# Depthwise convolution on TensorE in strips of 16 channels and two phases, with phases put back in order by on-chip transfers

## The reference, cut to what matters

```python
for i in range(4):                       # DEPTH, D_MODEL 1024, SEQ 2048, D_FF 2816
    if i % 2 == 0:                       # layers 0 and 2
        h = einsum('bsd,de->bse', x, w_in) + b_in
        val, gate = split(h, 2)
        h = val * sigmoid(gate)
        h = causal_depthwise_conv(h, w_dw)  # width 31
        h = silu(layer_norm(h + b_dw, ln_g, ln_b))
        mix = einsum('bsd,de->bse', h, w_out) + b_out
    else:                                # layers 1 and 3
        mix = (trailing means over 2, 4, 8, 16 positions - x) @ w_grp, scaled
    x = layer_norm(alpha * x + mix)
    x = layer_norm(alpha * x + swiglu(x))
```

## Time and profile before

| what | us |
|---|---|
| median of 3 runs | 2491.88 |
| lowest, highest | 2471.06, 2785.29 |
| the profiled execution | 2470.84 |
| its span (slowest core, 2) | 2469.3 |
| spans of the 8 cores | 2450.0 to 2469.3 |
| PE busy in the span | 2393.7 |
| DVE, ACT, POOL busy | 1532.0, 1115.2, 216.5 |

### The profile page before, as it was taken

How to read it: one execution, slowest core, us unless ns; L and a number is a source line. 1 busy time by engine, 2 the same in 40 slices (tenths; PEclk the granted TensorE clock), 3 DMA queues, 4 the chain that set the end, 5 groups by cost and what they waited for, 6 DMA issues and landing times.

```text
span 2469.3 us, 32261 instructions; the slowest of 8 cores (2450.0 to 2469.3 us)
## 1 busy us (share of the span) xinstructions
PE 2393.7 (97%) x12412; PEld 1076.5 (44%) x12412; DVE 1532.0 (62%) x2372; ACT 1115.2 (45%) x1656; POOL 216.5 (9%) x410
## 2 busy tenths in 40 slices
PE   6988999999999999999999999999999999999996
PEld 2333344444444444444444444444444444444444
DVE  3457577468846883735774726764885588555255
ACT  3556445435353535364463554552636263624033
POOL 1000110000000010000100000001000001010110
PEclk9998999999999999999999999999999999999998
DMA  8895986444544454467744477654444435466653
GB/s 182 203 167 99 166 142 103 75 78 66 92 69 81 69 83 68 81 115 143 125 87 67 77 138 125 124 94 73 70 73 78 79 66 89 71 106 139 98 95 99
DMA packets 112456, 250.35 MB, mean 101 GB/s; under 512 B 12080, under 2 KB 55088, under 8 KB 112304
## 3 DMA queue, kind: packets, MB, share of 16 engines
q0 software_dynamic: 58464, 191.92, 47.0%
q1 hardware_dynamic: 53840, 56.38, 9.9%
HBM read 419.17 MB, written 16.78 MB: 177 GB/s over the span
## 4 chain that ended last, share of the span: by engine, by line
PE 89%; issue 6%; DMA 3%; DVE 1%; POOL 1%; SPq 0%; ACT 0%; DVEq 0%; POOLq 0%; ACTq 0%
PE ps L875 89%; DMA sb_R<-x 1%; DMA sb_x<-ud 1%; DMA sb_wM<-win 0%; DMA sb_wF<-wgu 0%; DMA ud<-sb_ust 0%; POOL sb_wM L346 0%; DVE sb_R L452 0%; DVE sb_R L454 0%; POOL sb_wF L346 0%; SPq L652 0%; ACT sb_xT L783 0%; POOL sb_R L774 0%; SPq L774 0%; DVE sb_lnQ L426 0%
## 5 line engine op out<-in xcount | busy, mean ns | idle before, releaser
L875 PE MATMUL ps<-sb_xT,sb_wF 128*128 128x512 bf16 x5632 | 1235.0, 380 | 4.5 <-ACT sb_xT L467 3.7
L875 PEld LDWEIGHTS ps<-sb_xT,sb_wF 128*128 128x128 bf16 x5632 | 550.0, 98 | 684.0 <-issue 24.8
L875 PE MATMUL ps<-sb_hT,sb_wF 128*128 128x512 bf16 x2640 | 582.6, 379 | 0.0
L553 DVE TENSOR_TENSOR sb_hT<-ps,sb_sgF 128x512 bf16<-128x512 f32 x352 | 243.0, 690 | 452.5 <-PE ps L875 441.9
L551 ACT ACTIVATE sb_sgF<-ps 128x512 f32<-128x512 f32 x352 | 210.0, 597 | 534.1 <-PE ps L875 527.5
L875 PEld LDWEIGHTS ps<-sb_hT,sb_wF 128*128 128x128 bf16 x2640 | 256.6, 98 | 317.8 <-issue 12.5
L417 ACT ACTIVATE sb_lnX<-sb_R 128x512 f32<-128x512 f32 (+1 forms) x231 | 140.6, 614 | 369.1 <-DVE sb_R L532 204.2
L532 DVE TENSOR_TENSOR sb_R<-sb_R,ps 128x512 f32<-128x512 f32 (+1 forms) x264 | 177.0, 670 | 165.5 <-PE ps L875 164.1
L875 PE MATMUL ps<-sb_xT,sb_wM 128*128 128x512 bf16 x1024 | 232.3, 385 | 25.4 <-ACT sb_xT L783 24.3
L346 POOL DMA_DIRECT2D sb_wF<-wgu x198 | 104.7, 529 | 1123.2 <-PE ps L875 1123.2
L478 ACT ACTIVATE sb_R<-sb_R,sb_cst 128x512 f32<-128x512 f32 (+1 forms) x256 | 192.6, 797 | 7.4 <-DVE sb_R L454 6.9
(11 more groups left out here) (85 smaller groups left out, 1299.2 us busy)
## 6 DMA issues: line engine op xcount, KB each, us to landing
sb_wF<-wgu POOLq DMA_DIRECT2D x198, 512.0 KB, 5.1
sb_wF<-wd POOLq DMA_DIRECT2D x120, 352.0 KB, 4.4
sb_x<-ud SPq DMA_DIRECT2D x192, 135.0 KB, 5.9
sb_wM<-win POOLq DMA_DIRECT2D x32, 512.0 KB, 7.4
sb_wM<-wout POOLq DMA_DIRECT2D x32, 512.0 KB, 6.4
ud<-sb_ust SPq DMA_DIRECT2D x64, 128.0 KB, 5.7
y<-sb_R SPq DMA_DIRECT2D x12, 512.0 KB, 8.7
sb_R<-x SPq DMA_DIRECT2D x8, 512.0 KB, 16.6
```

Of the source, the lines that this page charges most:

```text
L553: S.op("dve", lambda e: e.tensor_tensor(out=hT[:, jj, h * NT:(h + 1) * NT], in0=ps[:, bu, :], in1=sgF[:, i, :], op=ALU.mult), reads=[("PS" ...
L875: r = self.e.matmul(*a, **k)
```

## The change

A tap tile is now made of two phases, even and odd positions. The 128 rows of contraction are 2 input phases times 4 shifts times 16 channels; the 32 output columns are 16 channels times 2 output phases. So a strip has 16 channels, there are 8 strips (four side by side, two halves h), and a strip needs 4 steps of 256 columns: 32 matmuls a tile as before, with half the columns.

- DVE writes ust by phase and puts 15 positions of history ahead of each row (three kinds: zeros, from the tile before, from uh). The store writes both phases; ud has a row of its own for each quarter.
- x4 is filled by two loads, one per input phase. Each has the source pattern [1, 4], [8 XW, 16], [1, 8 XW - 4]: four shifts by one element of 16 channels.
- Results stand by (channel, phase) on partitions. ACT evicts each half apart; the norm (`phase_finish`) adds the two halves on DVE, and its matmuls have 256 columns. Silu is two operations per block, and two on-chip transfers per block, issued by SP, put the phases side by side along the row. `conv_out` reads that copy, and DVE adds it to R with a strided view of PSUM.
- Tap weights come in their own tensor `lag` in bf16, by two loads on POOL. The last 16 columns of pooling history move into x4's third buffer.
- A write waits for the readers of a buffer alone where there are any, no more for the last writer too.

```diff
-XW = NT + 28
+XW = NH + 16
...
-            if w in self.last_w:
+            if self.readers.get(w):
+                deps.extend(self.readers[w])
+            elif w in self.last_w:
                 deps.append(self.last_w[w])
-            deps.extend(self.readers.get(w, ()))
...
+            s_, q_, sk, qk = sums(st)
+            for t, k in ((s_, sk), (q_, qk)):
+                S.op("dve", lambda e, t=t: e.tensor_tensor(out=t[:, 0:NH], in0=t[:, 0:NH], in1=t[:, NH:NT],
+                                                           op=ALU.add), reads=k, writes=k, dur=tt(NH))
...
+                e.matmul(ps[:, bm, 0:NH], samem, s_, start=True, stop=True)
+                return e.matmul(ps[:, bq, 0:NH], samem, q_, start=True, stop=True)
...
+                j = (i + 2) % 3
+                S.op("dve", lambda e: e.tensor_copy(out=head, in_=ust[:, j, :, NH:NH + 15]),
+                     reads=[("US", j)], writes=[("UX", i)], dur=0.1)
+            S.op("dve", lambda e: e.scalar_tensor_tensor(
+                out=ust[:, i, :, 15:15 + NH].rearrange("p f n -> p n f"),
+                in0=tgt[:].rearrange("p (n f) -> p n f", f=2), scalar=1.0,
+                in1=vbt[:].rearrange("p (n f) -> p n f", f=2), op0=ALU.add, op1=ALU.mult),
+                reads=[("TG",), ("VB",)], writes=[("US", i)], dur=DV)
...
-            for s in range(4):
-                o = q * NT - 28 - s
-                z = max(0, -o)
-                src = ud[L][c, :, o + z:o + XW].rearrange("(g p) w -> p g w", g=4)
-                S.op("sp", lambda e, s=s, z=z, src=src: e.dma_start(out=x4[s * 32:(s + 1) * 32, i, :, z:XW],
-                                                                    in_=src),
...
+            for f in range(2):
+                row = ud[L][f, c, q]
+                src = bass.AP(row.tensor, row.offset, [[1, 4], [8 * XW, 16], [1, 8 * XW - 4]])
+                S.op("sp", lambda e, f=f, src=src: e.dma_start(out=x4[f * 64:(f + 1) * 64, i, 0:8 * XW - 4], in_=src),
+                     reads=[("UD", L, c, q)], writes=[("X4", i, f)], dma=f"d_x4_{i}_{f}", dur=0.55, size=277000, lat=3.0)
...
+                for h in range(2):
+                    for m in range(4):
+                        for g in range(4):
+                            ins = e.matmul(ps[g * 32:(g + 1) * 32, b, h * NH:(h + 1) * NH], wt[:, m * 8 + 2 * g + h, :],
+                                           x4[:, i, (2 * g + h) * XW + 12 - 4 * m:(2 * g + h) * XW + 12 - 4 * m + NH],
+                                           start=(m == 0), stop=(m == 3))
...
+                for f in range(2):
+                    src = bass.AP(yb.tensor, yb.offset + f * step, [[2 * step, 64], [NH, 2], [1, NH]])
+                    S.op("sp", lambda e, f=f, src=src: e.dma_start(
+                        out=yb[:, NT + f * NH:NT + (f + 1) * NH], in_=src),
+                        reads=[tk], writes=[dk], dma=f"{yt[3]}{c}_{f}", dur=0.55, size=65536)
...
+                rv = rq(c, q).rearrange("p (n f) -> p n f", f=2)
+                S.op("dve", lambda e, b=b, rv=rv: e.tensor_tensor(
+                    out=rv, in0=rv, in1=ps[:, b, :].rearrange("p (f n) -> p n f", f=2), op=ALU.add),
```

More of the change, by code:

```diff
@@ L201, in _columns @@
     add("b2", 8 * DEPTH)
-    add("sel", 32)
+    add("sel", 16)
     add("ones", 128)
+    add("same", 128)
     add("invc", 16)
@@ L206, in _columns @@
         add(f"bin{l}", 16)
[L207 to L210, removed]
+        add(f"bdw{l}", 16)
+        add(f"lng{l}", 16)
+        add(f"lnb{l}", 16)
         add(f"bout{l}", 8)
@@ L621, in conv_in @@
             i = flip("ust", 3)
[L622 to L626, removed]
+            head = ust[:, i, :, 0:15]
+            if q == 0:
+                S.op("dve", lambda e: e.memset(head, 0.0), writes=[("UX", i)], dur=0.1)
+            elif q == 2:
+                S.op("dve", lambda e: e.tensor_copy(out=head, in_=uh[:, c, :, 0:15]),
+                     reads=[("UH", c)], writes=[("UX", i)], dur=0.1)
+            else:
+                j = (i + 2) % 3
[6 more added lines that the diff above has]
+                reads=[("TG",), ("VB",)], writes=[("US", i)], dur=DV)
+            S.op("sp", lambda e: e.dma_start(
+                out=ud[L][:, c, q].rearrange("f k (g w) -> (k g) f w", g=8), in_=ust[:, i]),
+                reads=[("US", i), ("UX", i)], writes=[("UD", L, c, q)], dma=f"d_us{i}", dur=0.45, size=139264, lat=1.0)
+            if q == 1:
+                S.op("dve", lambda e: e.tensor_copy(out=uh[:, c, :, 0:15], in_=ust[:, i, :, NH:NH + 15]),
+                     reads=[("US", i)], writes=[("UH", c)], dur=0.1)
         def conv_taps(q, L, c, bk, yt):
@@ L668, in conv_taps @@
+                return ins
+            S.op("pe", mm, reads=[("X4", i, s) for s in range(2)] + wk, writes=[("PS", b)], dur=1.1)
+            for h in range(2):
+                S.op("act", lambda e, h=h: e.activation(out=y[:, h * NH:(h + 1) * NH], in_=ps[:, b, h * NH:(h + 1) * NH],
+                                                        func=AF.Identity, bias=col(f"bdw{l}", 2 * c + h), scale=1.0),
+                     reads=[("PS", b), ("C0",)], writes=yk[h:h + 1], dur=0.48)
             ln_acc(bk["st"], c, y, yk, (yt[0][0], yt[2][0]))
@@ L673, in out @@
             def out(c):
-                S.op("act", lambda e: e.activation(out=yt[1][c], in_=yt[0][c], func=AF.Silu,
-                                                   bias=col(f"lnb{l}", c), scale=col(f"lng{l}", c)),
-                     reads=yt[2][c] + [("C0",)], writes=yt[2][c], dur=0.86, table="silu")
-            ln_finish(bk["st"], [(yt[0][c], yt[2][c]) for c in range(8)], bk["ln"], out)
+                y, yb, (tk, dk) = yt[0][c], yt[1][c], yt[2][c]
+                for h in range(2):
+                    S.op("act", lambda e, h=h: e.activation(
+                        out=yb[:, h * NH:(h + 1) * NH], in_=y[:, h * NH:(h + 1) * NH], func=AF.Silu,
+                        bias=col(f"lnb{l}", 2 * c + h), scale=col(f"lng{l}", 2 * c + h)),
+                        reads=[tk, ("C0",)] if h == 0 else [tk, dk, ("C0",)], writes=[tk], dur=0.5, table="silu")
+                step = yb.ap[0][0]
+                for f in range(2):
[3 more added lines that the diff above has]
+                        reads=[tk], writes=[dk], dma=f"{yt[3]}{c}_{f}", dur=0.55, size=65536)
+            phase_finish(bk["st"], [(yt[0][c], yt[2][c]) for c in range(8)], bk["ln"], out)
         def conv_out(q, L, bk, yt):
@@ L712, in pool_head @@
                 rk = [*RK(2 * g, q), *RK(2 * g + 1, q)]
-                pk = [("X4", i, s) for s in range(4)]
+                pk = [("X4", i, s) for s in range(2)]
                 if q == 0:
@@ L847, in build @@
         consts()
+        S.op("dve", lambda e: e.memset(ust[:, :, :, XW - 1:XW], 0.0), writes=[("UX", i) for i in range(3)], dur=0.1,
+             boost=9 * BOOST)
         ringM.load()
@@ L950, in _prep @@
     m["cst"] = cst
+    m["lag"] = lags
     for L in layers:
```

119 lines of the change are left out of this document (77 added, 42 removed).

## The result

The changed kernel is slower: a ratio of 1.0421 (95% interval 1.0363 to 1.0479), with a median of 2592.24 us against 2483.96 us for the kernel before. Its profiled execution took 2576.41 us, 1.5 us more than its span, as before. The forecast was 2507 us, "within 2%" its likeliest single outcome. The time lies in the range for 8 in 10 (2415 to 2620), but outside the 2468 to 2560 that the forecast gave for itself, and close to rival 1's 2598. In some executions the cores of one die ran slower, at a lower granted clock than the others: the ratios leave such executions out and the medians do not, and since one die was like that in the profiled execution of three experiments (the product alone, and four engines in one layer only), their rows are of cores of the other die, which are named.

A forecast was written before the change was run, and what follows sets the result against it. PE was taken to bound the dense part, with tap loads on four DMA engines deciding. 2470.84 + 3.6 (dense: 42.3 stalls less 38.7 saved) + 32 (first 300 us) = 2506, say 2507 us; own range 2468 to 2560, 8 in 10: 2415 to 2620.

The forecast's parts named there:

- rival 1: Tap loads become the bound, four engines at only 18 GB/s, stalls 90 us: 2598 us, chance 0.22.
- What PE saves: Dense part: tap tile 1.84 to 1.02 us, 33.6 us over 41 tiles; norms 5.1 us; 38.7 us together.
- Rival 3: PE's issue is the limit and the tap tile stays at 1.84 us; 2466 us with spread loads, chance 0.06.
- Four engines: Tap loads, outermost source count 4, lie on four DMA engines: 139 KB each, 5.8 us a tile at 24 GB/s.
- Rival 2: Tap loads spread over 16 engines, no stall added, dense part gains 38.7 us: 2422 us, chance 0.28.
- The stalls of the dense part: PE waits for tap loads in five groups behind 300 us: 6.9 + 7.8 + 9.9 + 7.8 + 9.9 = 42.3 us.
- the formula: Eight-tile group's loads need 5T + 3 = 41.5 us at T = 7.7 us; PE's large matmuls give 31.6 to 34.6 us.
- The first 300 us: Between 60 and 300 us, weights 131, tap tiles 133, stores some 8: 272 us of DMA demand against 240.
- +32 us: Time added before 300 us, because the four engines' 272 us of loads and stores exceed 240 us.
- 32 + 10 = 42: First stage: 32 us longer on four engines; some 10 us saved there under rival 2's spread loads.
- All this is covered by PE: Added ACT and DVE work, strided forms at 0.69 us included, hides behind PE, with ACT at 45% and DVE at 62%.
- The reorders, priced at nothing: 128 on-chip transfers issued by SP: same number of SP issues, norm tail some 6 us longer, PE order has room.

The follow-up runs named there:

- the product alone: Changed kernel with one edit: the DVE product walks its output phase by phase, tap loads still on four engines; ratio 1.0411 to the kernel before.
- four engines in one layer only: Two kernels, changed kernel with tap loads of layer 0 on 16 engines and layer 2 on four, and the mirror; ratios 1.017 and 1.0128, medians 2536.00 and 2529.41 us.
- the kernel with spread loads: Changed kernel with one edit: tap loads name the 16 channels outermost, so 16 engines, product still slow; median 2445.66 us, ratio 0.9888.
- half-load: Changed kernel, product mended, phase 0 tap loads with shifts outermost (4 engines), phase 1 with channels (16); median 2483.53 us, ratio 1.005.
- two-engine runs: Changed kernel, product mended, four tap loads per tile, each with two shifts outermost; median 2886.17 us, ratio 1.1674.
- the one with both edits: Changed kernel with the product written phase by phase and tap loads over 16 engines; median 2424.42 us, ratio 0.9798.

## Why the prediction was right, and where it was not

- **What PE saves: right.** The tile holds PE 0.99 us (1188.84 to 1189.83 below), against 1.02. Behind the mark the 40 tiles went from 76.4 us of busy time to 42.3 and the norms from 70.9 to 66.3 (the kernel with spread loads): 34.1 + 4.6 = 38.7 us, the term of the sum. Rival 3 falls.
- **Four engines: right**, by the packet counts and times and by the run with spread loads. Rival 2's case is that run: it was given 2422 us and took 2446, or 2424 with the product mended.
- **The stalls of the dense part: right in size**, 42.9 us for 42.3. That the rate was 24 GB/s agrees: a packet of 4344 B lasts 168 ns in the median and 190 in the mean over the records, 23 to 26 GB/s. Group by group the stalls are 7.6, 7.9, 6.3, 11.1 and 9.9 us, where the prediction had 6.9, 7.8, 9.9, 7.8 and 9.9: three fit, and the misses of the other two, 3.6 too few and 3.3 too many, cancel. So the closeness of the total is in part luck, and the formula's errors in the half-load and the two-engine runs, one each way, say the same.
- **What a stall costs: a term that was missing.** The dense part lost 81.0 us to four engines (2134.3 against 2053.3): 42.9 of waits for loads, 14.2 - 3.8 = 10.4 for vbt, 25.2 in PE's busy time for the same 10433 matmuls (2053.5 against 2028.3), and 2.5 of rest. The timeline of PE in the kernel after shows the 25 us being lost (start us, us, instruction, idle before):

```profile
1188.84 1.06 PE L949 MATMUL ps<-sb_x,sb_w 128*32 128x256 bf16 x32
1189.83 3.63 PE L949 MATMUL ps<-sb_xT,sb_wM 128*128 128x512 bf16 x16
...
1210.88 1.06 PE L949 MATMUL ps<-sb_x,sb_w 128*32 128x256 bf16 x32
1211.87 1.90 PE L949 MATMUL ps<-sb_xT,sb_wF 128*128 128x512 bf16 x8
1219.58 1.90 PE L949 MATMUL ps<-sb_x,sb_w 128*32 128x256 bf16 x32 [5.81 <-DMA sb_x<-ud]
1221.41 3.38 PE L949 MATMUL ps<-sb_xT,sb_wF 128*128 128x512 bf16 x8
```

  Behind a wait of 5.81 us the tile takes 1.90 us instead of 1.06, and eight large matmuls 3.38 instead of 1.90: 2.3 us more, at the lower clock level (1.2 GHz), as the clock of the two stretches shows (length, then PE, PEld, DVE, ACT, POOL, clock share, DMA share, GB/s):

```profile
1219.58:1221.41 1.83, 1.83 (x33) 1.22 (x33) 0.00 (x0) 0.00 (x0) 0.00 (x0) 0.50 0.26 106
1221.41:1223.00 1.59, 1.59 (x8) 0.58 (x5) 1.23 (x1) 1.39 (x3) 0.00 (x0) 0.50 0.25 104
```

  The granted clock of the whole dense part is 0.98 where it was 1.00. The Trainium skill, TensorE: Matmul & The Clock Gate (section on how oscillation bites in real kernels), warns of just this: a PE that idles for transfers comes back throttled. The trace agrees. I counted each stall once; this one costs its length and 2.3 us behind it.
- **The first 300 us: the step that failed**, "+32 us". On equal work it was +58. The step was a sum of shares of four DMA engines, 272 us of demand against 240, with the product at 0.69 us and covered. The run with the product alone mended is that very case, and it shows 428.3 - 382.6 = 45.7 us (353.4 + 29.2 = 382.6 is the mark before on equal work). So the loads alone were priced 14 us too low, and the slow product adds the other 12.3. The split depends on the order in which the two are mended, since they share one chain:

| first stage, mark on the core of the rows (mean of the cores) | us |
|---|---|
| four engines, product slow (after) | 440.6 (433.8) |
| four engines, product mended | 428.3 (427.2, undisturbed die) |
| 16 engines, product slow | 392.1 (383.4) |
| 16 engines, product mended | 372.1 (364.0) |

  The product costs 20.0 us with spread loads and 12.3 with four engines (19 and 7 in the means). Four engines cost 48.5 us with the slow product and 56.2 with the mended one (50 and 63), where the forecast implied 32 + 10 = 42. Both terms were mis-sized: the loads by 6 to 21 us, the product at 2.48 us where 0.69 was taken and double kept as the upper end. "All this is covered by PE" didn't hold where PE has gaps. The gain with both mended, 382.6 - 372.1 = 10.5 us, is just what rival 2 had (some 10).
- **The reorders, priced at nothing: wrong** by 11 to 17 us. They are paid with spread loads; what they cost beside four engines was not measured (PE waits for them 18.7 us in the kernel after and 7.6 us in the one with both edits).
- **The sum.** 2507 + 25 (clock) + 26 (first stage) + 14 (vbt, dense part) = 2572, of 2576 measured; the three added terms are read from these runs afterwards. The mechanism, four engines, was right, and three terms were missing or too small, all on the same side. That the time is still in the stated range is owed to the room kept for rival 1, which came out at 2598 by another way: 90 us of stalls at 18 GB/s, and there were 42.9 at 24. Its number was near, and its mechanism was not there. The kernel is slower for its loads (129.5 us between the spans, the clock behind their stalls included); the product counts for 9 to 26 us.

**Open.** Of the 48.5 us that four engines cost in the first stage I can't say how much is the late landing of the loads, how much that of the stores they depend on (10.5 against 4.5 us) and how much the clock (0.88 against 0.92); no run holds one of these fixed. Nor was it tried whether packing several reorders into one transfer wins their 11 to 17 us.

## What to carry to other kernels

Order a load's pattern so that the outermost count on both sides is 16, or a multiple of it; here, with 4 or 16 at the source, the order of two dimensions was worth some 130 us, more than all the saving on PE, and permuting a table of weights paid for it. Count a stall of PE at its length and the slow matmuls that can follow it (2.3 us behind one of 5.8 us here), and price a strided write by what it does per element, never at the price of the contiguous form. A covered engine is covered only where the bound engine is dense: price each edit once in the stretch that has gaps.

## What the runs showed of the hardware that I had not expected

- A DVE product of 512 columns whose bf16 output hops between two rows with every element takes 2477 ns. Written in runs, with the hop of two on both f32 inputs, it takes 694, the same as with no hop (690). The Trainium skill, Vector Engine (DVE) Microarchitecture Reference (measured stream behaviour), has 1.71 to 2.51 ns per column for an output of 4-byte words that hops or steps with every element; by it an estimate would be 0.9 to 1.3 us. The rows show 4.8 ns per column for this 2-byte output, so the measurement decides.
- SP's issue of a load slows down when the load lies on few engines: 594 ns in the median on 16, 2320 on two (with twice as many loads), up to 16.2 us. On four the median stays at 514 ns, but the longest is 8.5 us.
- Stores that are themselves spread land after 10.5 us instead of 4.5 when four engines carry all tap loads beside them.
